# DeltaNet scan: the inverse built in 32x32 blocks, block transposes on VectorE, block substitution for the last join

## The chip, the cores and the metric

The kernel runs on one NeuronCore of a Trainium2 chip. The metric is device time in microseconds (us) of one execution. The engines are named as in the profile: PE (TensorE matmul), PEld (TensorE's weight loads, which overlap PE), DVE (VectorE), ACT (ScalarE), POOL (GpSimd), SP (SyncE, which here issues DMAs).

## What is computed

Two layers of a hybrid block act on 1024 latent and 256 context tokens of width 1024. Each has four groups of heads side by side (windowed attention, DeltaNet, retention, latent attention), an output projection and an MLP. Only the DeltaNet group is touched. The reference computes it per head and per direction in chunks:

```python
def _delta_update(s, w_i, u_i, kt_i, gl_i):
    v_new = u_i - jnp.einsum('bhcd,bhde->bhce', w_i, s)
    s_new = s * jnp.exp(gl_i)[..., None, None] + jnp.einsum('bhcd,bhce->bhde', kt_i, v_new)
    return s_new, v_new

# gated_delta_chunked, per chunk:
decay = jnp.exp(jnp.where(incl, g_cum[..., :, None] - g_cum[..., None, :], -jnp.inf))
a_mat = jnp.where(strict, jnp.einsum('bhncd,bhnsd->bhncs', kb, k) * decay, 0.0)
lhs = a_mat + jnp.eye(c_, dtype=a_mat.dtype)
rhs = jnp.concatenate([kb * jnp.exp(g_cum)[..., None], v * beta], axis=-1)
wu = lax.linalg.triangular_solve(lhs, rhs, left_side=True, lower=True)
# scan over chunks:
s_new, v_new = _delta_update(s, w_i, u_i, kt_i, gl_i)
o_i = jnp.einsum('bhcd,bhde->bhce', qd_i, s) + jnp.einsum('bhcs,bhse->bhce', qk_i, v_new)
```

There are 4 heads of 64 channels and 2 directions. The kernel takes chunks of 128 tokens, so each layer has 10 chunks per direction (2 context, 8 latent).

## The kernel before

Each layer runs through phases separated by barriers of all engines; `dn_scan` is one of them. Every engine has its own `dn_scan`, and all of them walk one hand-written list, `scan_plan()` (line 590), of pieces (name, step `s_`, direction `q`, level `lv`). An engine issues its part of each piece in the order of that list and waits on semaphores (`u_...`) where it needs another engine's result. So the list is the order of the queue of every engine, and an instruction that waits holds all behind it on its engine.

A step handles one chunk for both directions and all four heads. For the two directions `q`:

- gsum (PE), arg (DVE, four `STT` at line 2439 with a mask), exp (ACT, line 1814): the decay matrix. gram (PE, line 1207): products k.k and q.k. at (DVE, lines 2448 and 2450): both times decay.
- first (POOL, lines 2852 and 2853), seed (PE): the start of the inverse of (I + A), held as two 64x64 diagonal blocks per head, as `lower` and as its transpose `upper`.
- five levels of y and u double the size of the solved blocks from 2 to 64. y (PE, line 1228; DVE masks the result at line 2453 into `step`) multiplies A with `lower`. u (PE) makes two products, line 1236 for `lower` and line 1239 for `upper`; ACT copies both back (lines 1819, 1821; at the last level line 1826 writes `inv`).
- x and z (PE, lines 1248 and 1259; ACT, lines 1832 and 1837) join the two 64x64 blocks into the full 128x128 inverse `inv`. The next step's y waits for it.
- keg (POOL), w (PE, line 1269; ACT, line 1841): the inverse times decayed keys. v (PE, lines 1275 to 1281): state times q, inverse times values, minus w times state. DVE scales both at lines 2456 and 2457.
- kept, kt (POOL), o (PE, lines 1288 and 1291), out (DVE, lines 2463 to 2465): state update and output, added into `d_o`.

The pieces w, v, o and out of step s run between the levels of step s+1, and gsum to first run a step ahead. All matmuls of the scan are f32; each leaves two records on PE and two on PEld. The blocks of the array that a matmul uses follow from its operands' partitions: y and u alternate between rows and columns 0 to 63 and 64 to 127.

Of the kernel before, what the change touches and what calls it, by code (L numbers as in the profile page):

```python
# [16 lines left out]
ALU = mybir.AluOpType  # L17
# [23 lines left out]
LEVELS = 7  # L41
SCAN_MASKS = 7
# [107 lines left out]
class Lane:  # L150
# [84 lines left out]
    "u_g", "u_arg", "u_dt", "u_gram", "u_first", "u_ymm", "u_ysb", "u_umm", "u_lower", "u_upper", "u_xmm", "u_xsb",  # L235
    "u_zmm", "u_full", "u_keg", "u_wmm", "u_wsb", "u_vmm", "u_vsb", "u_omm", "u_done", "u_at", "u_kt", "u_kept")]
# [5 lines left out]
def build(nc, d, book):  # L242

    with ExitStack() as ctx:
# [134 lines left out]
        levels, j1 = cut(Hn, j0, 2, SCAN_MASKS, 64)  # L379
# [20 lines left out]
        for q_ in range(2):  # L400
            b = {}
            for n_ in ("lower", "upper", "step", "first"):
                b[n_], r0_ = cut(ringf, r0_, H, 64)
            for n_ in ("at", "qkd", "inv"):
                b[n_] = []
                for _ in range(2):
                    half_, r0_ = cut(ringf, r0_, H, P)
                    b[n_].append(half_)
            for n_ in ("keg", "kt", "wt", "vn"):
# [180 lines left out]
        def scan_plan():  # L590
# [7 lines left out]

            both = lambda what, s_, lv=0: [(what, s_, 0, lv), (what, s_, 1, lv)]
            one = lambda what, s_, q: [(what, s_, q, 0)]  # L600
            plan = []
            for what in ("gsum", "arg", "exp", "gram", "at", "first"):
                plan += both(what, 0)
            plan += one("gsum", 1, 0) + both("seed", 0)
            for s_ in range(NT):
                late = lambda what, q: one(what, s_ - 1, q) if s_ else []
                soon = lambda what, q: one(what, s_ + 1, q) if s_ + 1 < NT else []
                then = lambda what, q: one(what, s_ + 2, q) if s_ + 2 < NT else []
                y, u = (lambda lv, w_=w_: both(w_, s_, lv) for w_ in "yu")
                plan += late("w", 0) + y(1) + late("w", 1) + late("kept", 0) + late("kept", 1) + soon("arg", 0)  # L610
                plan += late("v", 0) + soon("exp", 0) + u(1) + y(2) + late("o", 0) + both("keg", s_) + soon("gram", 0)
                plan += u(2) + late("out", 0) + soon("at", 0) + late("v", 1) + y(3) + soon("gsum", 1)
                plan += u(3) + soon("first", 0) + soon("arg", 1) + y(4) + soon("exp", 1) + late("o", 1) + soon("gram", 1)
                plan += u(4) + late("out", 1) + soon("at", 1) + y(5) + soon("first", 1) + u(5) + both("kt", s_)
                plan += then("gsum", 0) + soon("seed", 0) + [("x", s_, 0, 0)] + soon("seed", 1) + [("z", s_, 0, 0)]
            for what in ("w", "kept", "v", "o", "out"):
                plan += both(what, NT - 1)
            return plan

# [131 lines left out]
        def _(pe):  # L751
# [429 lines left out]
            def dn_scan():  # L1181
                blocks = [slice(0, 64), slice(64, P)]
                for what, s_, q, lv in scan_plan():
                    b, now, tile = sc[q], s_ % 2, scan_tiles[s_][q]
                    at_, inv, cols = b["at"][now], b["inv"][now], slice(tile * P, (tile + 1) * P)
                    pair, prod, tail = ps[:, q, :], ps[:, 2 + q, :], ps[:, 4 + q, :]
                    upper = b["first"] if lv == 1 else b["upper"]
                    of = lambda h: slice(h * 64, (h + 1) * 64)
                    if what == "gsum":

                        if s_:
                            pe.wait_ge(sems[f"u_at{1 - q}"], nth(f"u_at{1 - q}", s_ + q))
# [9 lines left out]
                    if what == "gram":  # L1202
                        pe.wait_ge(sems[f"u_arg{q}"], nth(f"u_arg{q}", s_ + 1))
# [4 lines left out]
                        m.then_inc(sems[f"u_gram{q}"], tally(f"u_gram{q}"))  # L1208
                    if what == "seed":
                        pe.wait_ge(sems[f"u_first{q}"], nth(f"u_first{q}", s_ + 1))  # L1210
                        if s_:
                            pe.wait_ge(sems[f"u_lower{q}"], nth(f"u_lower{q}", 6 * s_))
                            pe.wait_ge(sems[f"u_upper{q}"], nth(f"u_upper{q}", 5 * s_))
                        for h in range(H):
                            for r in blocks:
                                pe.matmul(pair[r, h * 64:(h + 1) * 64], b["first"][r, h, :], ident[r, r],
                                          start=(h == 0), stop=False, skip_group_check=True)
                        for r in blocks:
                            m = pe.matmul(pair[r, 256:512], ident[r, r], b["first"][r].rearrange("p h c -> p (h c)"),
                                          start=False, stop=False, skip_group_check=True)  # L1220
                        m.then_inc(sems[f"u_umm{q}"], tally(f"u_umm{q}"))
                    if what == "y":
                        if lv == 1 and s_:
                            pe.wait_ge(sems[f"u_full{q}"], nth(f"u_full{q}", s_))
                        pe.wait_ge(sems[f"u_lower{q}"], nth(f"u_lower{q}", 6 * s_ + lv))
                        for h in range(H):
                            for r in blocks:
                                m = pe.matmul(prod[r, of(h)], at_[r, h, r], b["lower"][r, h, :], start=True, stop=True, skip_group_check=True)  # L1228
                        m.then_inc(sems[f"u_ymm{q}"], tally(f"u_ymm{q}"))
                    if what == "u":  # L1230
                        pe.wait_ge(sems[f"u_ysb{q}"], nth(f"u_ysb{q}", 5 * s_ + lv))
                        if lv > 1:
                            pe.wait_ge(sems[f"u_upper{q}"], nth(f"u_upper{q}", 5 * s_ + lv - 1))
                        for h in range(H):
                            for r in blocks:
                                pe.matmul(pair[r, of(h)], upper[r, h, :], b["step"][r, h, :], start=False, stop=(lv == 5), skip_group_check=True)  # L1236
                        for h in range(H):
                            for r in blocks:
# [1788 lines left out]
```

## Time and profile before

| | us |
|---|---|
| median of 3 runs | 4048.92 (4048.8 to 4049.25) |
| the profiled execution | 4048.99 |
| its span | 4047.2 |
| scan of layer 0, from 766.1 to 1086.9 | 320.8 |
| scan of layer 1, from 2851.9 to 3172.3 | 320.4 |

The view by stretches gives the busy time of each engine in a stretch of time and, behind it, the number of instructions in the order PE, PEld, DVE, ACT, POOL (PE and PEld alone where it is asked for one line of matmuls), then the mean granted clock of TensorE (1.00 is full) and the DMA's share. The view in order of time merges instructions of one line that follow one another: start, length of the whole piece, engine, line, operation, count, and in brackets the idle time before it with what ended it. Since matmuls overlap, the time that a group takes from its queue is the distance from its start to the start of the next group.

### The profile page before, as it was taken

How to read it: one execution, taken by the hardware profiler on the slowest of the kernel's cores; microseconds unless marked ns; L12 is line 12 of the kernel's file. 1: busy time of each engine (PE TensorE's matmuls, PEld its weight loads, DVE VectorE, ACT ScalarE, POOL GpSimd, SP SyncE). 2: the span in 40 equal slices, each digit the busy share in tenths (PEclk: the TensorE clock that was granted, in tenths of full speed). 3: DMA queues.
4: the chain of work that ended last, by engine and by line, in shares of the span. 5: the costliest groups of instructions: out<-in, count | busy, mean ns of one | idle time of the engine just before them, and what ended most of it. 6: DMA issues, size and time to landing. Idle time of an engine off the chain costs nothing.

```text
span 4047.2 us, 75588 instructions
## 1 busy us (share of the span) xinstructions
PE 3825.9 (95%) x32478; PEld 3201.9 (79%) x32478; DVE 1951.6 (48%) x3457; ACT 1121.1 (28%) x2430; POOL 905.1 (22%) x659
## 2 busy tenths in 40 slices
PE   6999999899899999999998999999899899999997
PEld 5668888788787888888886668878788778888886
DVE  3455566444456333333357464565444564333446
ACT  3444242333413111111114452252333321000111
POOL 1000100122103333333322001100222034443442
PEclk8999999899899999999998999999999899999999
DMA  4230000100000101101111120001000101111111
GB/s 179 102 149 32 22 22 22 61 3 3 23 32 32 42 31 41 42 31 41 41 40 73 63 105 22 22 12 42 32 3 3 43 32 53 42 52 52 41 52 52
DMA packets 30518, 180.81 MB, mean 45 GB/s; under 512 B 2592, under 2 KB 7968, under 8 KB 15136
## 3 DMA queue, kind: packets, MB, share of 16 engines
q1 hardware_dynamic: 28944, 173.66, 11.7%
q8 instruction: 221, 3.62, 0.4%
q10 hardware_dynamic: 1296, 3.07, 0.2%
q14 instruction: 57, 0.47, 0.0%
HBM read 168.32 MB, written 8.39 MB: 44 GB/s over the span
## 4 chain that ended last, share of the span: by engine, by line
PE 85%; DVE 8%; ACT 4%; issue 2%; DMA 1%; POOL 1%; ACTq 0%; POOLq 0%; DVEq 0%; SPq 0%
PE ps L1364 37%; PE ps L768 9%; PE ps L778 8%; PE ps L803 4%; PE ps L901 3%; PE ps L1228 3%; PE ps L1236 2%; PE ps L1239 2%; PE ps L943 2%; PE ps L986 1%; PE ps L1317 1%; PE ps L1207 1%; PE ps L812 1%; PE ps L1291 1%; PE ps L1008 1%
## 5 line engine op out<-in xcount | busy, mean ns | idle before, releaser
L1364 PE MATMUL ps<-Yn_parts,ring_parts 128*128 128x512 f32 (+1 forms) x3888 | 798.9, 367 | 2.4 <-DVE Yn_parts L2610 2.1
L1364 PEld LDWEIGHTS ps<-Yn_parts,ring_parts 128*128 128x128 f32 x3888 | 671.2, 189 | 126.7 <-DVE Yn_parts L2610 5.4
L1364 PE MATMUL ps<-temp_parts,ring_parts 128*128 128x512 f32 (+1 forms) x2560 | 726.5, 369 | 5.0 <-DVE Hn_parts L2551 3.6
L2871 POOL TENSOR_TENSOR ring_parts<-ring,consts 128x2048 fp32r<-128x2048 f32 x62 | 286.5, 4621 | 1187.4 <-DMA ring<-in_ff 1187.4
L1364 PEld LDWEIGHTS ps<-temp_parts,ring_parts 128*128 128x128 f32 x2560 | 464.9, 189 | 88.0 <-DVE Hn_parts L2551 4.1
L768 PE MATMUL ps<-ring_parts,Xn_parts 128*128 128x256 f32 x2560 | 506.1, 293 | 24.1 <-DVE Hn_parts L2122 16.2
L2498 DVE SCALAR_TENSOR_TENSOR Xn<-ps,mods,Xn 128x256 f32<-128x256 f32 (+1 forms) x364 | 251.7, 692 | 574.2 <-PE ps L1364 504.3
L1364 PE MATMUL ps<-Hn_parts,ring_parts 128*128 128x512 f32 (+1 forms) x1280 | 471.4, 368 | 0.0
L768 PEld LDWEIGHTS ps<-ring_parts,Xn_parts 128*128 128x128 f32 x2560 | 418.4, 196 | 27.3 <-issue 22.6
L1926 ACT ACTIVATE Yn<-ps 128x256 f32<-128x256 f32 (+1 forms) x160 | 88.6, 554 | 1237.6 <-PE ps L1364 1237.6
L2609 DVE TENSOR_TENSOR Yn<-Yn 128x256 f32<-128x256 f32 (+1 forms) x160 | 191.3, 1196 | 402.7 <-ACT Yn_parts L1928 402.7
L768 PE MATMUL ps<-ring_parts,Hn_parts 128*128 128x256 f32 x1280 | 367.5, 287 | 0.0
L2872 POOL TENSOR_TENSOR ring_parts<-ring,ring_parts 128x2048 fp32r<-128x2048 f32 x62 | 291.7, 4704 | 4.9
L803 PE MATMUL ps<-consts,temp 128*128 128x128 f32 (+1 forms) x1416 | 231.1, 285 | 47.4 <-DVE temp L2151 15.7
L1364 PEld LDWEIGHTS ps<-Hn_parts,ring_parts 128*128 128x128 f32 x1280 | 241.6, 189 | 40.4
L803 PEld LDWEIGHTS ps<-consts,temp 128*128 128x128 f32 (+1 forms) x1416 | 162.9, 142 | 114.2 <-issue 54.7
L768 PEld LDWEIGHTS ps<-ring_parts,Hn_parts 128*128 128x128 f32 x1280 | 251.5, 197 | 0.8
L2453 DVE TENSOR_TENSOR ring<-ps,Hn 128x256 f32<-128x256 f32 x200 | 84.7, 423 | 228.3 <-PE ps L1228 226.6
L1819 ACT ACTIVATE ring<-ps 128x256 f32<-128x256 f32 x240 | 91.6, 382 | 331.6 <-PE ps L1239 302.2
L2610 DVE TENSOR_TENSOR Yn_parts<-Yn,Yn_parts 128x256 fp32r<-128x256 f32 (+1 forms) x160 | 179.5, 1122 | 5.5
L901 PE MATMUL ps<-Yn,temp 96*128 96x512 f32 (+1 forms) x400 | 153.7, 518 | 4.2 <-ACT temp L1640 2.7
L778 PE MATMUL ps<-Xn_parts,ring_parts 128*128 128x512 f32 (+1 forms) x576 | 153.6, 355 | 0.9 <-DVEq L211 0.9
(318 smaller groups left out, 5610.1 us busy)
## 6 DMA issues: line engine op xcount, KB each, us to landing
ring<-in_ff SPq DMA_DIRECT2D x64, 1024.0 KB, 4.7
ring<-in_ada SPq DMA_DIRECT2D x22, 2048.0 KB, 9.0
ring<-in_halves SPq DMA_DIRECT2D x28, 1024.0 KB, 4.8
Xn<-in_x SPq DMA_DIRECT2D x1, 5120.0 KB, 16.8
Hn<-in_ada SPq DMA_DIRECT2D x2, 2048.0 KB, 21.1
Xn<-in_x SPq DMA_DIRECT2D x2, 2048.0 KB, 18.5
kept_x<-Xn SPq DMA_DIRECT2D x4, 1024.0 KB, 4.5
Xn<-kept_x SPq DMA_DIRECT2D x1, 4096.0 KB, 15.5
```

The source lines that it names most:

```text
L768: m = pe.matmul(ps[:, bank, 0:256], (G_hi, H_lo)[a][:, k, t * P:(t + 1) * P], w[b][:, k, :], start=(k == 0 and part == 0), stop=(k == KT - ...
L778: m = pe.matmul(ps[:, bank, 0:hi - lo], w[a][:, k, j * P:(j + 1) * P], x[b][:, k, lo:hi], start=(k == 0 and part == 0), stop=(k == KT - 1 ...
L803: return pe.transpose(out, src, ident[0:rows, 0:rows])
L901: m = pe.matmul(m_flat[:, base + a:base + b], m_q[0:96, h, t * P:(t + 1) * P], m_k[0:96, h, a:b], start=True, stop=True, skip_group_check= ...
L1228: m = pe.matmul(prod[r, of(h)], at_[r, h, r], b["lower"][r, h, :], start=True, stop=True, skip_group_check=True)
L1364: m = pe.matmul(ps[:, bank, 0:hi - lo], w[a][:, k, j * P:(j + 1) * P], x[b][:, k, lo:hi], start=(k == 0 and part == 0), stop=(k == k_n - 1 ...
L1819: A(flat(b["lower"]), ps[:, q, 0:256], ACT.Copy).then_inc(sems[f"u_lower{q}"], tally(f"u_lower{q}"))
L2498: return STT(X[:, j, lo:hi], ps[:, bank, 0:hi - lo], mods[:, L, gate_ + j, which:which + 1], X[:, j, lo:hi], ALU.mult, ALU.add)
L2609: link(TT(u_, u_, u_, ALU.mult))
L2610: TT(U_lo[:, j, lo:hi], u_, U_hi[:, j, lo:hi].bitcast(F32), ALU.subtract).then_inc(sems["hidden"], tally("hidden"))
L2871: link(TT(by(half_hi[s]), by(half[s]), spread(ones, 1, HALF // P), ALU.mult))
L2872: TT(half_lo[s], half[s], half_hi[s].bitcast(F32), ALU.subtract).then_inc(sems["split"], tally("split"))
```

## The change

The 128x128 matrix of a chunk is now solved with 32x32 blocks. `level_masks` makes masks of 32 columns and five levels. Four levels of y and u remain, each with 16 matmuls of 32x32 per direction in place of 8 of 64x64. The four diagonal blocks of A are first packed by a new piece, pk (PE with ACT), and atm (POOL) multiplies them by the masks of all levels at once, so that y's result is only copied (ACT). u makes only `lower`; a VectorE transpose of 32x32 blocks makes `upper`. a and b (PE with ACT) join pairs of 32x32 blocks to 64x64; wide (DVE) writes the diagonal part. The second join to 128x128 is gone: reach takes state times k and state times q, the correction is subtracted from the values (DVE, then POOL), and x1, off, x2 do the substitution over the two 64x64 blocks directly on them. w, keg, and the inverse-times-value product are gone. arg moves from DVE to ACT (Relu with a bias and negative scale, then exp with scale -1); the triangle mask that it held is now applied by mask (POOL) to qkd. The accumulation into `d_o` moves from DVE to POOL (acc). `at` and `qkd` of direction 0 get a third buffer. The plan is written anew.

```diff
-LEVELS = 7
-SCAN_MASKS = 7
+LEVELS = 5
+SCAN_MASKS = LEVELS + 1
...
+    one = lambda what, s_, q, lv=0: [(what, s_, q, lv)] if 0 <= s_ < NT else []
+    part = lambda what, s_, q, heads=range(H): [i_ for h in heads for i_ in one(what, s_, q, h)]
     plan = []
+    for q in range(2):
+        plan += one("gsum", 0, q)
+    for q in range(2):
+        plan += part("arg", 0, q) + one("exp", 0, q) + one("gram", 0, q)
+    for q in range(2):
+        plan += part("at", 0, q) + one("qkd", 0, q) + one("mask", 0, q) + one("pk", 0, q) + one("atm", 0, q)
+    plan += one("gsum", 1, 0) + part("arg", 1, 0) + one("exp", 1, 0) + one("gram", 1, 0)
+    plan += both("start", 0) + both("seed", 0) + both("kept", 0) + both("kt", 0)
     for s_ in range(NT):
+        late = lambda what, q, s_=s_: one(what, s_ - 1, q)
+        soon = lambda what, q, s_=s_: one(what, s_ + 1, q)
+        then = lambda what, q, s_=s_: one(what, s_ + 2, q)
+        plan += y(1) + late("x1", 0) + late("x1", 1) + part("at", s_ + 1, 0)
+        plan += u(1) + late("off", 0) + late("off", 1) + soon("qkd", 0) + soon("mask", 0)
+        plan += y(2) + soon("pk", 0) + late("x2", 0) + late("x2", 1) + soon("gsum", 1)
+        plan += u(2) + part("arg", s_ + 1, 1, (0, 1)) + late("tail", 0) + soon("atm", 0)
+        plan += y(3) + part("arg", s_ + 1, 1, (2, 3)) + late("tail", 1)
+        plan += u(3) + soon("exp", 1) + soon("gram", 1)
+        if s_:
+            plan += both("kept", s_)
+        plan += y(4) + late("acc", 0) + late("acc", 1) + part("at", s_ + 1, 1, (0, 1)) + one("reach", s_, 0)
+        plan += u(4) + part("at", s_ + 1, 1, (2, 3)) + one("reach", s_, 1)
+        plan += [("a", s_, 0, 0)] + both("wide", s_) + soon("start", 0) + soon("qkd", 1) + soon("mask", 1) + soon("pk", 1) + soon("atm", 1) + then("gsum", 0)
+        plan += [("b", s_, 0, 0)] + soon("seed", 0) + part("arg", s_ + 2, 0) + soon("start", 1)
+        plan += soon("seed", 1) + then("exp", 0) + then("gram", 0)
+        if s_:
+            plan += both("kt", s_)
+    for what in ("x1", "off", "x2", "tail", "acc"):
     return plan
+blocks32 = [slice(32 * n_, 32 * n_ + 32) for n_ in range(4)]
+blocks64 = [slice(0, 64), slice(64, P)]
+def pair_of(q, c):
+    return (2 * c, 2 * c + 1) if q == 0 else (2 * c + 1, 2 * c)
+def kept_back(q):
+    return 3 - q
...
+            if what == "pk":
+                pe.wait_ge(sems[f"u_kq{q}"], nth(f"u_kq{q}", 2 * s_ + 2))
+                for r in blocks32:
+                    m = pe.matmul(ps[r, scan_banks(s_, q)[0], 0:P], ident[r, r], at_[r, :, r], start=True, stop=True, skip_group_check=True)
+                m.then_inc(sems[f"u_pk{q}"], tally(f"u_pk{q}"))
...
             if what == "y":
+                if lv == 1:
+                    pe.wait_ge(sems[f"u_staged{q}"], nth(f"u_staged{q}", 2 * s_ + 2))
+                    if s_:
+                        pe.wait_ge(sems[f"u_inv{q}"], nth(f"u_inv{q}", 2 * s_))
+                else:
+                    pe.wait_ge(sems[f"u_lower{q}"], nth(f"u_lower{q}", 4 * s_ + lv - 1))
                 for h in range(H):
+                    for r in blocks32:
+                        m = pe.matmul(prod[r, of32(h)], atm[r, lv, of32(h)], b["lower"][r, h, :], start=True, stop=True, skip_group_check=True)
                 m.then_inc(sems[f"u_ymm{q}"], tally(f"u_ymm{q}"))
             if what == "u":
+                pe.wait_ge(sems[f"u_ysb{q}"], nth(f"u_ysb{q}", 4 * s_ + lv))
                 if lv > 1:
+                    pe.wait_ge(sems[f"u_upper{q}"], nth(f"u_upper{q}", 4 * s_ + lv - 1))
                 for h in range(H):
+                    for r in blocks32:
+                        upper = atm[r, 0, of32(h)] if lv == 1 else b["upper"][r, h, :]
+                        m = pe.matmul(pair[r, of32(h)], upper, b["step"][r, h, :], start=False, stop=(lv == 4), skip_group_check=True)
+                m.then_inc(sems[f"u_umm{q}"], tally(f"u_umm{q}"))
+            if what == "a":
+                for q_ in range(2):
+                    pe.wait_ge(sems[f"u_lower{q_}"], nth(f"u_lower{q_}", 4 * s_ + 4))
+                    for h in range(H):
+                        for c in range(2):
+                            near, far = (blocks32[n_] for n_ in pair_of(q_, c))
+                            m = pe.matmul(ps[far, 2 + q_, of32(h, P)], sc[q_]["at"][s_ % kept_back(q_)][near, h, far],
+                                          sc[q_]["lower"][near, h, :], start=True, stop=True, skip_group_check=True)
+                    m.then_inc(sems[f"u_lmm{q_}"], tally(f"u_lmm{q_}"))
...
+            if what == "reach":
+                if s_:
+                    pe.wait_ge(sems[f"u_tv{q}"], nth(f"u_tv{q}", 4 * s_))
+                else:
+                    pe.wait_ge(sems["u_packed1"], nth("u_packed1", 1))
+                for a_ in (1, 0):
+                    for j in range(2):
+                        m = pe.matmul(tail[:, 256 * a_ + j * P:256 * a_ + (j + 1) * P], raw[:, 2 * a_ + j, cols], b["S"][:, j, :],
+                                      start=True, stop=True, skip_group_check=True)
+                m.then_inc(sems[f"u_tmm{q}"], tally(f"u_tmm{q}"))
+            if what == "x1":
+                pe.wait_ge(sems[f"u_r{q}"], nth(f"u_r{q}", s_ + 1))
+                pe.wait_ge(sems[f"u_inv{q}"], nth(f"u_inv{q}", 2 * s_ + 2))
                 for h in range(H):
+                    m = pe.matmul(tail[have, of(h)], inv[have, h, :], b["r"][have, of(h)], start=True, stop=True, skip_group_check=True)
+                m.then_inc(sems[f"u_tmm{q}"], tally(f"u_tmm{q}"))
...
+            if what == "arg":
+                if lv == 0:
+                    act.wait_ge(sems[f"u_g{q}"], nth(f"u_g{q}", s_ + 1))
+                    if s_:
+                        act.wait_ge(sems[f"u_kq{q}"], nth(f"u_kq{q}", 2 * s_))
+                at_col = gate_col(q, tile)
+                m = A(b["ex"][:, lv, :], ps[:, scan_banks(s_, q)[lv // 2], (lv % 2) * P:(lv % 2 + 1) * P], ACT.Relu,
+                      bias=g_tok[:, lv, at_col:at_col + 1], scale=-1.0)
+                if lv == H - 1:
+                    m.then_inc(sems[f"u_decay{q}"], tally(f"u_decay{q}"))
...
+            if what == "y":
+                act.wait_ge(sems[f"u_ymm{q}"], nth(f"u_ymm{q}", 4 * s_ + lv))
+                A(flat(b["step"]), ps[:, 2 + q, 0:P], ACT.Copy).then_inc(sems[f"u_ysb{q}"], tally(f"u_ysb{q}"))
...
+            if what == "x1":
+                act.wait_ge(sems[f"u_tmm{q}"], nth(f"u_tmm{q}", 5 * s_ + 2))
+                A(b["vn"][have], ps[have, 4 + q, 0:256], ACT.Copy, scale=-1.0).then_inc(sems[f"u_x1{q}"], tally(f"u_x1{q}"))
 ...
+            if what == "u":
+                dve.wait_ge(sems[f"u_lower{q}"], nth(f"u_lower{q}", 4 * s_ + lv))
+                dve.transpose(flat(b["upper"]), flat(b["lower"])).then_inc(sems[f"u_upper{q}"], tally(f"u_upper{q}"))
+            if what == "wide":
+                dve.wait_ge(sems[f"u_upper{q}"], nth(f"u_upper{q}", 4 * s_ + 4))
+                if s_:
+                    dve.wait_ge(sems[f"u_tmm{q}"], nth(f"u_tmm{q}", 5 * s_ - 1))
+                TT(b["inv"].rearrange("p h (n c) -> p h n c", n=2), spread(b["upper"], 2, 2), spread(in_pair, 1, H), ALU.mult)\
+                    .then_inc(sems[f"u_wide{q}"], tally(f"u_wide{q}"))
...
+            if what == "off":
+                dve.wait_ge(sems[f"u_tmm{q}"], nth(f"u_tmm{q}", 5 * s_ + 3))
+                TT(b["r"][off], tail[off, 256:512], b["r"][off], ALU.add).then_inc(sems[f"u_tv{q}"], tally(f"u_tv{q}"))
...
+            if what == "mask":
+                pool.wait_ge(sems[f"u_kq{q}"], nth(f"u_kq{q}", 2 * s_ + 2))
+                TT(qkd, qkd, spread(tri[:, q, :], 1, H), ALU.mult).then_inc(sems[f"u_mask{q}"], tally(f"u_mask{q}"))
+            if what == "atm":
+                pool.wait_ge(sems[f"u_packed{q}"], nth(f"u_packed{q}", s_ + 1))
+                if s_ >= 2:
+                    pool.wait_ge(sems[f"u_ymm{q}"], nth(f"u_ymm{q}", 4 * s_ - 4))
+                link(TT(hd(atm[:, 0, :]), b["pk"], spread(levels[:, q, 0, :], 1, H), ALU.mult))
+                TT(hd(atm[:, 0, :]), hd(atm[:, 0, :]), spread(levels[:, q, LEVELS, :], 1, H), ALU.add).then_inc(sems[f"u_staged{q}"], tally(f"u_staged{q}"))
+                TT(atm[:, 1:LEVELS, :].rearrange("p l (h c) -> p l h c", h=H), spread(b["pk"], 1, LEVELS - 1), spread(levels[:, q, 1:LEVELS, :], 2, H), ALU.mult)\
+                    .then_inc(sems[f"u_staged{q}"], tally(f"u_staged{q}"))
+            if what == "reach":
+                pool.wait_ge(sems[f"u_tv{q}"], nth(f"u_tv{q}", 4 * s_ + 1))
+                TT(b["r"], kv_tok[:, tile, 256:512], b["r"], ALU.subtract).then_inc(sems[f"u_r{q}"], tally(f"u_r{q}"))
...
```

The scan plan of the kernel before is line 599 to 618; `late`, `soon` and `then` mean that a piece belongs to the step before, the next and the one after.

## Rows read from the trace of the kernel before

**Rows 1.** The page's first part: busy us (share of the span) xinstructions of each engine.

```profile
PE 3825.9 (95%) x32478; PEld 3201.9 (79%) x32478; DVE 1951.6 (48%) x3457; ACT 1121.1 (28%) x2430; POOL 905.1 (22%) x659
```

**Rows 2.** Busy time by stretch: length, then us and instructions of each engine, clock, DMA.

```profile
766.10:1086.90 320.80, 301.01 (x6640) 267.55 (x6640) 141.04 (x400) 113.89 (x320) 79.53 (x122) 0.98 0.01 3
...
832.50:863.70 31.20, 29.81 (x664) 26.48 (x664) 14.01 (x40) 11.40 (x33) 7.89 (x12) 1.00 0.01 3
...
767.50:777.70 10.20, 7.73 (x61) 5.54 (x62) 5.05 (x17) 1.64 (x3) 5.25 (x8) 0.50 0.00 1
...
2851.90:3172.30 320.40, 300.64 (x6640) 267.39 (x6640) 141.21 (x400) 113.87 (x320) 79.48 (x122) 0.98 0.01 3
```

**Rows 3.** In order of time, one steady step of layer 0: start, us, engine, line, operation.

```profile
832.50 0.78 ACT L1837 ACTIVATE ring<-ps 64x256 f32<-64x256 f32 x2 [0.67 <-PE ps L1259]
...
838.60 0.55 PEld L1239 LDWEIGHTS ps<-ring 64*64 64x64 f32 x16
...
839.07 0.55 PEld L1228 LDWEIGHTS ps<-ring 64*64 64x64 f32 x16
...
839.77 0.54 PEld L1228 LDWEIGHTS ps<-ring 64*64 64x64 f32 x16 [0.15 <-ACT ring L1819]
...
840.38 0.31 PEld L1288 LDWEIGHTS ps<-Yn 128*64 128x64 f32 x8
...
840.77 0.97 PEld L1291 LDWEIGHTS ps<-Yn,ring 128*128 128x128 f32 x8
...
841.80 0.73 PEld L1207 LDWEIGHTS ps<-temp 64*128 64x128 f32 x8
...
842.87 0.54 PEld L1236 LDWEIGHTS ps<-ring 64*64 64x64 f32 x16 [0.33 <-issue]
...
863.68 0.38 ACT L1837 ACTIVATE ring<-ps 64x256 f32<-64x256 f32 x1 [0.67 <-PE ps L1259]
```

**Rows 4.** Stretches of 25 ns at L1073 and L1160 alone, and of 0.48 us at seed.

```profile
420.32:420.35 0.03, 0.02 (x4) 0.02 (x4) 1.00 0.00 0
...
743.53:743.55 0.03, 0.02 (x4) 0.03 (x4) 1.00 3.83 1638
...
860.59:861.07 0.48, 0.48 (x30) 0.48 (x28) 0.00 (x0) 0.24 (x1) 0.48 (x2) 1.00 0.00 0
```

**Rows 5.** Groups by line and shape: count | busy us, mean ns of one | idle before.

```profile
L1228 PE MATMUL ps<-ring 64*64 64x64 f32 x3200 | 125.3, 221 | 2.2 <-ACT ring L1819 1.2
...
L1684 ACT ACTIVATE temp<-ps 128x128 f32<-128x128 f32 x20 | 5.5, 277 | 47.2 <-PE ps L803 47.2
...
L1589 ACT ACTIVATE temp<-ps,params 128x128 f32<-128x128 f32 x60 | 19.6, 362 | 11.5 <-PE ps L803 11.5
...
L2165 DVE TENSOR_SCALAR temp<-temp 128x128 f32<-128x128 f32 x20 | 4.2, 218 | 2.9 <-PE ps L803 2.9
...
L2448 DVE SCALAR_TENSOR_TENSOR ring<-ps,Hn 128x128 f32<-128x128 f32 x160 | 45.0, 343 | 15.2 <-DVE temp L2465 10.3 <-PE ps L1207 4.9
...
L2450 DVE TENSOR_TENSOR ring<-ps,Hn 128x512 f32<-128x512 f32 x40 | 27.1, 679 | 0.0
...
L2456 DVE TENSOR_TENSOR Yn<-ps,Hn 128x256 f32<-128x256 f32 x40 | 17.0, 424 | 70.1 <-PE ps L1281 70.1
...
L2853 POOL TENSOR_TENSOR ring<-ring,Hn 128x256 f32<-128x256 f32 x40 | 29.0, 725 | 3.1
```

**Rows 6.** In order of time, the first step of layer 0: weight loads of a seed.

```profile
774.91 0.93 PEld L1216 LDWEIGHTS ps<-consts,ring 64*64 64x64 f32 x16 [0.22 <-issue]
```

**Rows 7.** In order of time, layer 0: the first y, the last z and the end.

```profile
777.93 0.70 PEld L1228 LDWEIGHTS ps<-ring 64*64 64x64 f32 x16
...
1076.72 0.78 ACT L1837 ACTIVATE ring<-ps 64x256 f32<-64x256 f32 x2 [0.94 <-PE ps L1259]
...
1086.37 0.42 DVE L2465 TENSOR_TENSOR temp<-temp,Yn 128x256 f32<-128x256 f32 x1
```

More of the change, by code:

```diff
@@ L401, in build @@
             b = {}
-            for n_ in ("lower", "upper", "step", "first"):
-                b[n_], r0_ = cut(ringf, r0_, H, 64)
-            for n_ in ("at", "qkd", "inv"):
+            for n_ in ("lower", "upper", "step", "pk"):
+                b[n_], r0_ = cut(ringf, r0_, H, 32)
+            b["inv"], r0_ = cut(ringf, r0_, H, 64)
+            b["atm"] = []
+            for _ in range(2):
+                half_, r0_ = cut(ringf, r0_, LEVELS, P)
+                b["atm"].append(half_)
+            for n_ in ("at", "qkd"):
                 b[n_] = []
@@ L613, in scan_plan @@
[L613 to L616, printed above, removed]
+                late = lambda what, q, s_=s_: one(what, s_ - 1, q)
+                soon = lambda what, q, s_=s_: one(what, s_ + 1, q)
@@ L1211, in dn_scan @@
                         if s_:
[L1212 to L1217, printed above, removed]
@@ L1252, in dn_scan @@
-                    if what == "z":
-                        for q_ in range(2):
-                            pe.wait_ge(sems[f"u_xsb{q_}"], nth(f"u_xsb{q_}", s_ + 1))
-                            pe.wait_ge(sems[f"u_upper{q_}"], nth(f"u_upper{q_}", 5 * s_ + 5))
-                        for h in range(H):
-                            for q_ in range(2):
-                                have, off = blocks[q_], blocks[1 - q_]
-                                m = pe.matmul(ps[have, 2 + q_, of(h)], sc[q_]["step"][off, h, :], sc[q_]["inv"][now][off, h, off],
-                                              start=True, stop=True, skip_group_check=True)
-                                if h == H - 1:
-                                    m.then_inc(sems[f"u_zmm{q_}"], tally(f"u_zmm{q_}"))
@@ new lines, in dn_scan @@
+                    if what == "x2":
+                        pe.wait_ge(sems[f"u_tv{q}"], nth(f"u_tv{q}", 4 * s_ + 2))
+                        for h in range(H):
+                            m = pe.matmul(tail[off, of(h)], inv[off, h, :], b["r"][off, of(h)], start=True, stop=True, skip_group_check=True)
+                        m.then_inc(sems[f"u_tmm{q}"], tally(f"u_tmm{q}"))
+                    if what == "tail":
+                        pe.wait_ge(sems[f"u_tv{q}"], nth(f"u_tv{q}", 4 * s_ + 3))
@@ new lines, in dn_scan @@
+                    if what == "qkd":
+                        if s_ >= back:
+                            dve.wait_ge(sems[f"u_tmm{q}"], nth(f"u_tmm{q}", 5 * (s_ - back) + 5))
+                        TT(by_half(qkd), gram[:, :, 0, :, :], by_half(b["ex"]), ALU.mult).then_inc(sems[f"u_kq{q}"], tally(f"u_kq{q}"))
+                    if what == "start":
+                        dve.wait_ge(sems[f"u_staged{q}"], nth(f"u_staged{q}", 2 * s_ + 1))
+                        if s_:
+                            dve.wait_ge(sems[f"u_lmm{q}"], nth(f"u_lmm{q}", 2 * s_ - 1))
+                        dve.transpose(flat(b["lower"]), b["atm"][s_ % 2][:, 0, :]).then_inc(sems[f"u_start{q}"], tally(f"u_start{q}"))
```

285 lines of the change are left out of this document (113 added, 172 removed).

## The prediction

> **What bounds the kernel now.** I read the page first: PE is busy for 95% of the span [rows 1]. That share is over all stages, so I went to the stretches next. The change touches only the two DeltaNet scans. They fill 320.8 us (layer 0) and 320.4 us (layer 1), 641 of 4047 us, and in both PE is busy for 94% at a granted clock of 0.98 [rows 2]. In a steady stretch from one evacuation of z (ACT L1837) to the next, 832.50 to 863.68, a step takes 31.2 us, of which PE is busy for 29.8, DVE for 14.0, ACT for 11.4 and POOL for 7.9 [rows 2, 3]. So inside the scan the end is set by PE's own queue, and the other three have more than half of the step free. What I need from the trace is therefore how long PE takes for each kind of group, start to start, because a matmul's own duration overlaps the next one's.
>
> **PE's prices, from starts in one step [rows 3].** Each matmul of f32 data leaves two records. Sixteen 64x64 records, which alternate between two diagonal blocks of the array, take 839.07-838.60 = 0.47 us: 29 ns a record, 58 ns a record on one block. The o part of one direction (L1288, L1291) takes 841.80-840.38 = 1.42; its eight 128x128 records take 841.80-840.77 = 1.03, with the change of shape behind them. A gram (L1207) takes 842.87-841.80 = 1.07, with the change of shape behind it. A y group that is followed by another shape takes 840.38-839.77 = 0.61 in place of 0.47, so a change of shape costs about 0.15. A gsum has half of a gram's columns: (1.07-0.15)/2+0.15 = 0.6. At these prices a step before has ten y 4.7, ten u (two products each) 9.3, o 2.8, gram 2.1 and gsum 1.2, 20.1 of the 29.8 us; seeds, x, z, w and v are the rest.
>
> **The unknown price: 32x32 matmuls.** Nothing in the scan before is 32x32. Three rows bound it [rows 4]. L1073 uses four blocks of 32 rows: four matmuls start within 25 ns. L1160 uses four blocks of 32 columns: again four within 25 ns. And where seed and x overlap on all four 64x64 blocks, 28 weight loads fall into 0.48 us, 17 ns a record. So different blocks of the array run side by side, in rows and in columns, and a start itself costs about 6 ns (25/4). A 32-column record on one block should take half of the 58 ns, and four blocks at once give 7 to 8 ns a record. Low end 0.22 us for a y or u group of 32 records, high end 0.93 (the 29 ns of the 64x64 pairs), with 17 ns (0.54) between them. I take 0.26, nearest to L1073, which has the same four row blocks. Pk and seed (8 records of 128 columns) I take at 0.3.
>
> **PE's list after the change, one step, both directions.** Removed: a fifth level of y and u, the second product of every u (the transpose that DVE now makes), x and z as 64x64, w, and the inverse-times-value part of v. Added: y and u as 32x32, 16 x 0.26 = 4.2 (before 14.0). a and b, 4 x 0.26 = 1.0. pk and seed, 4 x 0.3 = 1.2. x1, off and x2, six groups of eight 64x64 records on one block each, 6 x 0.47 = 2.8. reach, 2 x 1.03 = 2.1. tail as o before, 2.8. gsum 1.2, gram 2.1. Twelve further changes of shape, 12 x 0.15 = 1.8. Sum 19.2 us against 29.8. PE no longer fills the step, so what matters next is where its queue, which is strictly in the order of the plan, stops for others.
>
> **The new waits.** I walked the order of the plan with durations of ACT 0.28 (128x128 copy, L1684), 0.36 (with a bias operand, L1589), DVE 0.34 (L2448), 0.68 (L2450), 0.42 (L2456), POOL 0.73 per 256 elements (L2853) and 0.2 us from the last start of a PE group to its reader (one 64x64 record lasts 0.22, L1228) [rows 5]. Four places wait:
> The gram two steps ahead, directly behind b and the seeds, needs the four arg activations, which now are ACT's and stand behind b's four evacuations: 0.43+0.04+4x0.28+4x0.36 = 3.0 us after b begins, while PE has about 1.0 of b and seeds: 2.1 (y of the next step and everything else queue behind it).
> pk of direction 0 stands ahead of x2 and needs qkd, behind both off additions on DVE: 0.42+0.42+0.68 against PE's off and y groups: 0.6.
> pk of direction 1 stands ahead of b and needs qkd of direction 1, behind DVE's reach (2x0.42), wide (2x0.42), start (0.3) and qkd (0.68): 2.7 plus drain 0.2 and leftovers of two transposes, less PE's a group: 2.5. This holds b, thus the inverse, thus the next step.
> gsum behind it needs pk's evacuation by ACT: 0.6.
> Sum 5.8, so 25.0 at full clock. The 32x32 transposes by VectorE aren't in the trace; their nearest rows are 0.22 (L2165) and 0.34 (L2448), and I take 0.29. The eight of the levels come 2 to 4 us before they are needed; three lie on the third wait, so the ends move the step by -0.2 to +0.2. ACT's 38 and DVE's 36 instructions of a step, at 0.28 to 0.68 us each, come to about 13 and 12 us; POOL's, by elements, to about 13 (mask 2x1.3, atm 2x2.2, eight others at 0.7). All stay below 25: none becomes the bound, and what POOL newly does (mask, atm, reach's subtraction, acc) is covered by PE's middle levels as long as a step is longer than that. The change of ring buffers moves no DMA.
>
> **The clock.** The granted clock was 0.50 from 767.5 to 777.7, where PE was busy for 7.7 of 10.2 us with pauses for the others before and inside, and the sixteen 64x64 weight loads of a seed took 0.93 us there, against 0.55 for sixteen of y at full clock [rows 2, 3, 6]. The steps after that, with PE busy without a break, ran at 1.00. The new step has a stretch of some 5 us around b with little on PE in every step, so I expect the clock to fall to the 1.2 GHz level there and to come back during the first levels. The price runs from 0 to 3 us a step (the 3 us of gram, y, x1 and u after the pause taking twice as long); I take half: 1.5. Step: 26.5 us.
>
> **The sum.** Per layer: start to first y 12.7 (before, 766.1 to 777.9: 11.8; plus mask and atm on POOL); first step without late parts 26.5-6 = 20.5; seven at 26.5 = 185.5; the ninth without gsum, arg and gram ahead 23.0; the last without any look-ahead 17.5; the last tail 8.5 (before, 1076.7 to 1086.8: 10.1) [rows 2, 7]. Together 267.7 against 320.7, -53.0 a layer, -106 in all. The profiled execution took 4048.99 us for a span of 4047.2, the median of the runs is 4048.92, so the sum needs no shift: 4049-106 = 3943 us. Each us of the step is 20 us.
>
> **Rivals.**
> *Fewer waits (faster).* ACT's and DVE's short instructions overlap their predecessor, so the first and third wait shrink by about 3 us in all, and the clock stays at 1.00: step 22, 3853 us. For: the rows give how long one such instruction lasts, not how closely independent ones follow. Against: what PE waits for is the end of the last one.
> *Clock low for half of PE's work.* 19.2/2 = 9.6 us more, of which the 5.8 of waits hide somewhat over half: step 30, 4013 us.
> *PE takes 32x32 records no faster than 64x64 pairs (slower than before).* At 29 ns a record, y, u, a and b cost 11.7 more: step 36.7, with the clock kept up by a busy PE, 4147 us. It decides from a step of 31.8, that is 6.8 us over 25.0, or 12 ns more for each of the 576 records: about 20 ns a record. For: no row shows a longer run than 17 ns a record. Against: [rows 4].
> The Trainium skill has a rule that speaks for this rival: "TensorE: Matmul & The Clock Gate", Part 1, says that the starts of matmuls don't come closer than about 25 ns however small they are. By that figure a group of 32 would be 0.8 us, the step about 34 and the time, as an estimate, about 4100. The traces disagree with it where blocks differ: four starts in 25 ns [rows 4].
> *No change.* It needs a step of 31.4 to 32.2 by chance of the above.
>
> **Chances.** Forecast (step 24 to 29) 62%, fewer waits 15%, low clock 11%, slow 32x32 9%, no change 3%. A measurement of this kernel can tell about 0.2% (8 us) from no change. From the same cases: faster 87%, same 3%, slower 10%. The range reaches from the fewer-waits case to past the low-clock case, 3855 to 4030, and leaves out the slow 32x32 case and the best end.
>
> **What would show it.** Right: in a steady step, y and u groups start 0.2 to 0.3 us apart; PE's idle time is released by ACT (arg before gram, pk before gsum) and by DVE (qkd before pk), most of it around b; PE busy falls to about three quarters; the clock row of the scan falls below 0.98. Wrong: a y group of 0.5 us or more; idle PE in front of u or y in the middle levels (then the copies or transposes are the chain); POOL as releaser of start, y or x1.

## The result, and the profile after

The changed kernel takes 4020.18 us (median of 5 runs, 4013.82 to 4027.17), the one before 4049.25 (4048.8 to 4050.17) beside it: a ratio of 0.9929, 95% interval 0.9914 to 0.9943. So it is faster by 0.7%, which is clear of the noise, and inside the range, but by 29 us in place of 106. The profiled execution took 4017.37 us for a span of 4015.6.

The busy times of the page (of all stages), beside [rows 1]:

```profile
PE 3729.1 (93%) x33918; PEld 3083.6 (77%) x33918; DVE 1924.5 (48%) x3377; ACT 1116.2 (28%) x2550; POOL 986.6 (25%) x731
```

By stretch, as in [rows 2]: the scan of layer 0 (first gsum to last instruction), a long and a short step of it (from one first y to the next), the scan of layer 1:

```profile
768.90:1078.30 309.40, 256.07 (x7360) 210.09 (x7358) 125.13 (x360) 111.58 (x380) 120.83 (x160) 0.72 0.01 3
835.29:868.50 33.21, 28.95 (x739) 24.02 (x737) 12.62 (x36) 11.20 (x38) 12.07 (x16) 0.60 0.02 3
901.64:928.10 26.46, 21.69 (x739) 17.38 (x737) 12.43 (x36) 11.12 (x38) 12.07 (x16) 0.89 0.02 4
2837.20:3140.90 303.70, 251.40 (x7360) 206.83 (x7358) 125.04 (x360) 111.30 (x380) 120.81 (x160) 0.73 0.01 3
```

The two scans take 309.4 and 303.7 us, before 320.8 and 320.4. The granted clock of the scan, 0.98 before, is 0.72. The same step, with the same instructions, takes 26.5 us at a clock of 0.89 and 33.2 at 0.60. From one first y to the next, the second to eighth step of layer 0 take 26.6, 33.2, 33.2, 26.5, 28.9, 33.2 and 28.0 us: mean 29.9 (layer 1: 26.2 to 33.2, mean 29.7).

PE in order of time in the ninth step, which has no gsum and gram two steps ahead, from the end of the levels to the next first y (L1242 gram, L1265 y, L1302 reach, L1274 u, L1282 a, L1247 pk, L1292 b, L1254 seed), as in [rows 3] but for the matmuls:

```profile
1030.38 0.75 PE L1274 MATMUL ps<-ring 32*32 32x32 f32 x64
1031.06 1.14 PE L1242 MATMUL ps<-temp 64*128 64x256 f32 x8
1032.13 0.75 PE L1265 MATMUL ps<-ring 32*32 32x32 f32 x64
1032.81 1.16 PE L1302 MATMUL ps<-Hn,temp 128*128 128x128 f32 x8
...
1038.58 0.31 PE L1247 MATMUL ps<-ring,consts 32*32 32x128 f32 x4 [2.31 <-DVE ring L2498]
...
1041.21 0.65 PE L1254 MATMUL ps<-ring,consts 32*32 32x128 f32 x8 [1.65 <-DVE ring L2503]
```

Both directions of a y or u, 64 records, take 0.68 us to the next group (1031.06-1030.38, 1032.81-1032.13). Less 0.15 for the change of shape that is 0.27 a group, forecast 0.26. Around b PE is idle for 2.31 us, then for 1.65.

What PE waited for in layer 0, from 780 to 1080 us (us in total, times, longest):

```profile
PE ps L1247 <- DVE ring L2498: 20.9, 10, 2.3
PE ps L1242 <- ACT Hn L1857: 11.1, 9, 1.4
PE ps L1265 <- issue: 4.6, 7, 1.3
PE ps L1234 <- ACT ring L1868: 3.5, 9, 0.4
PE ps L1274 <- issue: 2.9, 4, 1.3
PE ps L1254 <- DVE ring L2503: 2.5, 4, 1.6
```

The places are those forecast: pk behind qkd, gram behind arg, gsum behind pk's evacuation. Seed behind start, and pauses that nothing in the profile explains ("issue") inside y and u groups, are new. Groups of layer 0 that the prediction had priced from [rows 5] (us, mean ns of one):

```profile
L2506 DVE STREAM_TRANSPOSE ring<-ring 128x128 f32<-128x128 f32 x80 | 23.8, 306 | 44.1 <-ACT ring L1874 42.2
...
L2511 DVE TENSOR_TENSOR ring<-ring,Hn 128x256 f32<-128x256 f32 x20 | 12.8, 682 | 0.0
```

The transposes take 0.306 us (forecast 0.29). Wide takes 12.8/20 = 0.64 (forecast 0.42).

### The profile page after: what moved, and what is told of

Same layout as the page of the kernel before. It is cut to its first block, busy times and chain, and to the rows that moved or that the text cites. A ratio compares the mean times of both kernels' runs of the same rounds, so it can differ in the third digit from the quotient of the medians.

```text
span 4015.6 us, 78630 instructions
## 1 busy us (share of the span) xinstructions
PE 3729.1 (93%) x33918; PEld 3083.6 (77%) x33918; DVE 1924.5 (48%) x3377; ACT 1116.2 (28%) x2550; POOL 986.6 (25%) x731
## 4 chain that ended last, share of the span: by engine, by line
PE 83%; DVE 9%; ACT 5%; issue 2%; DMA 1%; POOL 1%; ACTq 0%; DVEq 0%; POOLq 0%; SPq 0%
PE ps L1402 38%; PE ps L803 9%; PE ps L813 8%; PE ps L838 4%; PE ps L936 3%; PE ps L978 2%; PE ps L1242 2%; PE ps L1274 2%; PE ps L1265 1%; PE ps L1329 1%; PE ps L1302 1%; PE ps L1355 1%; PE ps L1021 1%; PE ps L1043 1%; PE ps L847 1%
## 5 line engine op out<-in xcount | busy, mean ns | idle before, releaser
L1402 PE MATMUL ps<-temp_parts,ring_parts 128*128 128x512 f32 (+1 forms) x2560 | 727.1, 370 | 5.0 <-DVE Hn_parts L2616 3.6
L2563 DVE SCALAR_TENSOR_TENSOR Xn<-ps,mods,Xn 128x256 f32<-128x256 f32 (+1 forms) x364 | 251.8, 692 | 572.7 <-PE ps L1402 501.7
L2271 DVE TENSOR_REDUCE small<-ps 128x1 f32<-128x1280 f32 x72 | 98.8, 1373 | 79.2 <-PE ps L936 78.9
L813 PE MATMUL ps<-temp_parts,ring_parts 128*128 128x512 f32 (+1 forms) x448 | 129.5, 374 | 0.0
## 6 DMA issues: line engine op xcount, KB each, us to landing
Hn<-in_ada SPq DMA_DIRECT2D x2, 2048.0 KB, 20.7
```

The costliest lines, as they stand in the source:

```text
L813: m = pe.matmul(ps[:, bank, 0:hi - lo], w[a][:, k, j * P:(j + 1) * P], x[b][:, k, lo:hi], start=(k == 0 and part == 0), stop=(k == KT - 1 ...
L1402: m = pe.matmul(ps[:, bank, 0:hi - lo], w[a][:, k, j * P:(j + 1) * P], x[b][:, k, lo:hi], start=(k == 0 and part == 0), stop=(k == k_n - 1 ...
L2271: dve.tensor_reduce(rowneg[:, at_], m_flat[:, base:base + latent_keys(t) * P], AX.X, ALU.min).then_inc(sems["rowmax"], tally("rowmax"))
L2563: return STT(X[:, j, lo:hi], ps[:, bank, 0:hi - lo], mods[:, L, gate_ + j, which:which + 1], X[:, j, lo:hi], ALU.mult, ALU.add)
```

## The experiments

The first theory was that PE's idle time around b lets the clock fall, and that the clock is the whole loss. Its rivals: the 32x32 work itself keeps the clock low ("small blocks", later "narrow"), or the waits themselves are the loss. A filler is matmuls of constants into PSUM columns that nobody reads; "wide" work is matmuls over more of the array than 32x32 blocks (the DVE piece wide is something else). Each kernel was timed against the one before, which took 4049 to 4051 us each time; the clock and the length are those of layer 0's scan in the profiled execution.

| | us | ratio, 95% interval | scan, us | clock |
|---|---|---|---|---|
| the change | 4020.2 | 0.9914 to 0.9943 | 309.4 | 0.72 |
| e1_fill_gaps | 3962.0 | 0.9764 to 0.9797 | 283.0 | 0.89 |
| e4_fill_elsewhere | 4081.8 | 1.0065 to 1.0098 | 337.8 | 0.71 |
| e2_qkd_early | 4031.3 | 0.9933 to 0.9966 | 316.3 | 0.62 |
| e3_qkd_early_gram_late | 3953.3 | 0.9735 to 0.9784 | 268.3 | 0.82 |
| e7_gram_late | 4017.4 | 0.9893 to 0.9926 | 308.7 | 0.68 |
| e8_qkd_fill_y1 | 3974.8 | 0.9797 to 0.9829 | 284.7 | 0.81 |
| e5_fill_narrow | 4123.8 | 1.0158 to 1.0219 | 354.9 | 0.74 |
| e9_fill_blocks | 3985.7 | 0.9821 to 0.9857 | 296.2 | 0.82 |
| e6_qkd_gram_fill | 3917.6 | 0.9657 to 0.9689 | 251.8 | 0.93 |
| e10_fill_gsum_only | 3933.5 | 0.9677 to 0.9723 | 261.6 | 0.87 |

**Filler in the idle stretches, and the same filler elsewhere.**

```diff
+if what == "fill":
+    for n_ in range(lv):
+        pe.matmul(ps[:, q, 384:512], ident, ident, start=True, stop=True, skip_group_check=True)
 # e1, in the plan
-... + soon("pk", 1) + ...
+... + soon("fill", 0, 8) + soon("pk", 1) + ...
-... + then("gram", 0)
+... + then("fill", 0, 5) + then("gram", 0)
 # e4 instead (into bank 2)
-u(3) + ...
+u(3) + soon("fill", 1, 13) + ...
```

> Thirteen f32 matmuls of 128x128 into unused PSUM columns are put into the two longest idle stretches of PE in a steady step: eight ahead of pk of direction 1, five ahead of gram two steps ahead (0.26 us each at full clock; they end later than the idle times of 2.3 and 1.4 us by little). Theory 'idle PE around b lets the clock fall': the scan stretch goes from a granted clock of 0.71 to 0.95 or more, the mean step from 29.2 to about 26.4 us, the time to about 3970 us, although PE has more to do. Rival 'small blocks': the 32x32 work itself lets the clock fall, so the clock stays below 0.8 and the time is 4020 to 4050 us. Rival 'waits': the loss is in the length of the waits, and the time stays at 4020 us or more whatever the clock does.

> The same thirteen matmuls as in the one that fills the two idle stretches, but all behind u of level 3, where PE does not wait. Theory 'idle PE around b lets the clock fall': the idle stretches stay, the clock still falls in each step (0.65 to 0.8), and the time grows by the filler, 18 x 3.4 to 5 us: 4080 to 4110 us. Rival 'small blocks': what matters is how much wide work PE has in a step, wherever it is; the clock rises as much as in the other kernel with filler.

In e1 the second filler opens an accumulation in a bank where a seed is open, which changes the inverse; PE's instructions are otherwise those of the change. A step of e1 (busy time by stretch):

```profile
935.00:960.30 25.30, 22.65 (x780) 19.18 (x776) 12.31 (x36) 11.13 (x38) 12.08 (x17) 1.00 0.01 4
```

With 3.3 us more of work the step takes 25.3 us, less than any of the change's seven middle steps in either layer (26.2 and more), at a clock of 1.00; the time falls by 58 us against the change. The clock of the whole scan, 0.89, is less than the 0.95 expected. Behind u of level 3 the same work costs 62 us. So the loss hangs on the clock, and on what PE does around b. "Waits" as the whole of the loss falls, and so does "small blocks" in the form that the amount of wide work decides.

**The waits taken away by order alone.**

```diff
 # e2
-u(4) + part("at", s_ + 1, 1, (2, 3)) + one("reach", s_, 1)
-[("a", ...)] + both("wide", s_) + soon("start", 0) + soon("qkd", 1) + soon("mask", 1) + soon("pk", 1) + ...
+u(4) + part("at", s_ + 1, 1, (2, 3)) + soon("qkd", 1) + soon("mask", 1) + one("reach", s_, 1)
+[("a", ...)] + both("wide", s_) + soon("start", 0) + soon("pk", 1) + ...
 # e7 (e3 is both)
-soon("seed", 1) + then("exp", 0) + then("gram", 0)
+soon("seed", 1)
-y(1) + late("x1", 0) + ...
+y(1) + (soon("exp", 0) + soon("gram", 0) if s_ else []) + late("x1", 0) + ...
```

> The product qkd of direction 1 (and its mask) goes ahead of DVE's reach, wide and start pieces, so that pk of direction 1 no longer waits for it; no work is added or left out. Theory 'idle PE around b lets the clock fall': the 2.1 us wait at pk goes, 18 steps x 2.1 = 38 us, and the clock rises with it; 3920 to 3980 us, scan clock 0.8 or more. Rival 'waits': only the wait goes, 3982 us, clock as it was (0.71). Rival 'next in line': the wait moves to seed, which waits for start on DVE; over 4000 us.

> As the one with qkd early, and exp and gram of direction 0 two steps ahead move behind the y of the next step's first level, so that this y is not queued behind ACT's arg. Theory 'idle PE around b lets the clock fall': both waits go (2.1 + 1.2 us a step) and the clock is 0.9 or more; step 23 to 25 us, 3870 to 3940 us. Rival 'waits': 18 x 3.3 = 59 us less, 3960 us, clock about 0.71. Rival 'next in line': DVE gets at of direction 0 later, its transposes for u queue behind it, and y of the middle levels waits; 3980 us or more.

> Exp and gram of direction 0 two steps ahead move behind the y of the next step's first level, qkd stays where it is: the half of the two moves that the earlier kernel with both left untold. Theory 'idle': the 2.3 us wait at pk stays, so the clock falls in each step as in the changed kernel; 18 steps x 1.2 us of the arg wait are gained, about 4000 us. Theory 'narrow': what matters is that wide work (gram, x1) follows soon after b; the clock comes back within a few us in each step, 0.9 in the scan, 3960 to 3985 us.

E2 comes out at 4031. That is what "next in line" has (over 4000), and the wait at seed does grow, from 2.5 to 8.4 us, but the time isn't lost there: the wait at pk went as meant, and the waits are shorter in all. PE's waits in e2, layer 0:

```profile
PE ps L1254 <- DVE ring L2503: 8.4, 18, 1.4
PE ps L1234 <- ACT ring L1868: 6.2, 9, 0.7
PE ps L1242 <- ACT Hn L1857: 2.5, 8, 0.5
PE ps L1247 <- DVE ring L2498: 2.0, 9, 0.2
```

19.1 us together, in place of the change's 38.0 in the same four (20.9+11.1+3.5+2.5), and still it is slower than the change by some 11 us, because the clock now falls at b in every step and stays there (three stretches in a row of e2, from the seeds behind b to y of the fourth level, then to the next seeds, then again):

```profile
892.60:916.50 23.90, 22.96 (x560) 18.79 (x556) 8.00 (x24) 8.13 (x27) 8.71 (x12) 0.50 0.01 3
916.50:923.40 6.90, 5.63 (x203) 4.63 (x192) 5.24 (x13) 3.08 (x12) 3.56 (x5) 0.99 0.01 2
923.40:947.20 23.80, 22.89 (x551) 18.67 (x546) 7.89 (x24) 8.15 (x27) 8.73 (x12) 0.50 0.01 3
```

PE is busy for 22.96 of 23.90 us, 96%, and the clock stays at 1.2 GHz; it returns behind the two tails and gram and is lost again at the next b. The middle steps take 30.8 to 31.3 us. So idle time doesn't explain why the clock stays low. The Trainium skill, "TensorE: Matmul & The Clock Gate", Part 1, says that "the default state is throttled, and activity releases the throttle"; in this stretch 23 us of matmuls did not.

The change itself shows both returns. Of its sixteen falls at b ahead of the second to ninth steps (both layers), the clock was back after 6.8 us in eight, after 10.2 in two, and after 23.9 to 30.7 in six. Two of them, with the same groups of work behind b:

```profile
831.45:855.35 23.90, 22.62 (x540) 18.64 (x544) 7.66 (x24) 8.25 (x28) 8.15 (x11) 0.50 0.01 3
896.30:903.13 6.83, 5.51 (x131) 3.65 (x127) 1.44 (x5) 3.40 (x11) 3.26 (x6) 0.50 0.01 2
```

They differ in where among these groups the clock fell. In the eight short ones the gram that follows b began 2.5 to 3.8 us after the fall, in the six long ones 1.8, 2.2, 3.9, 4.3, 4.5 and 7.5 us after it. In e2, with less waiting ahead of that gram, it began 0.5 to 1.8 us after each of the sixteen falls, and all sixteen took 23.9 us. This is read from the traces afterwards; no run shifted the fall alone, so it isn't shown to be the cause.

E7 shortens the arg wait but leaves the other: 4017, no gain, clock 0.68. Its "narrow" expectation missed, and "idle" was too hopeful by 17 us. Of the runs that only move work, e3 with both moves alone brings the clock up, to 0.82, and is 67 us faster. E3's 3953 us misses "idle" (at most 3940, clock 0.9) and lies 7 us from "waits" (3960), though not at the clock of 0.71 that this had: what the order alone gained and what the clock gave back aren't separated in e3.

**Wide work where PE doesn't wait, and narrow work where it does.**

```diff
 # e8: e2, and (into bank 0, start=False)
-y(1) + late("x1", 0) + ...
+y(1) + soon("fill", 0, 4) + late("x1", 0) + ...
 # e5: as e1 with 118 and 73 of
+r = blocks32[n_ % 4]
+pe.matmul(ps[r, 0, 384:416], ident[r, r], ident[r, r], start=False, stop=False, ...)
 # e9: as e1, each of 8 and 5 being
+for r in blocks32:
+    pe.matmul(ps[r, 0, 384:512], ident[r, r], ident[r, :], start=False, stop=False, ...)
```

> Qkd early alone (which ran at a clock of 0.61 with little idle time of PE), and four 128x128 matmuls into unused PSUM columns behind the y of level 1, where PE does not wait (1.0 us at full clock). Theory 'narrow': the clock, which there stays at 1.2 GHz for 24 us of narrow work in each step, is back soon after b; step 24.5 to 26 us, 3940 to 3970 us, although PE has 1 us more to do. Theory 'idle': no idle time is filled, so the clock stays at 0.61 and the time is 18 x 2 us longer, about 4070 us.

> The two idle stretches of PE (ahead of pk of direction 1 and of gram two steps ahead) are filled as long as in the kernel with thirteen wide matmuls, but with 32x32 ones on four blocks of the array: 118 and 73 of them, about 2.1 and 1.3 us at 8.8 ns a record. Theory 'idle': with PE as busy as there, the clock is as high (0.95 or more in the scan) and the time about 3960 us. Theory 'narrow': what counts is not only that PE is busy but with how wide work; the clock stays below 0.85 and the time is 4000 us or more.

> The two idle stretches of PE are filled once more, eight and five times, each time with four matmuls of 128 columns on the four diagonal 32x32 blocks of the array in place of one of 128x128. They run side by side, so a set should last about as long as one wide matmul (0.26 to 0.35 us), and 52 more matmuls a step don't strain PE's supply of instructions as the 191 small ones did. Theory 'idle': PE is as busy as with the wide filler, so the clock is 0.95 or more in the scan and the time 3960 to 3980 us. Theory 'narrow': a quarter of the rows and columns in use doesn't do; clock below 0.85, 4010 us or more.

E8 adds 1 us of work a step to e2, fills no wait, and is 57 us faster. A step of e8:

```profile
860.50:885.60 25.10, 21.04 (x744) 17.35 (x744) 12.91 (x37) 11.15 (x39) 12.31 (x17) 1.00 0.01 4
```

It is 5 us above "narrow" and 95 below "idle". Fourteen of its fifteen falls at b ahead of the second to ninth steps ended after 3.4 to 10.2 us, one after 23.9. In ten of them gram began 0.1 to 1.8 us after the fall, as in e2, and nine of these ten were over after 3.4 or 6.8 us: so here it is the added work behind b that brought the clock back soon. That it has to be wide isn't shown, since no run put as much narrow work in this place. E5 fits the ranges of "narrow", but doesn't decide as it was meant to: with 191 more small matmuls a step PE paused in the filler itself, with nothing in the profile to wait for (layer 0, first line of its waits), so the stretches were not filled:

```profile
PE ps L1228 <- issue: 31.2, 20, 2.5
```

E9 is the cleaner form. Its time lies between the two expectations, its clock, 0.82, under the 0.85 of "narrow". Around a, fill, pk, gsum and seed it holds the clock; then, in six of the sixteen steps, it is lost later, in pk or x2 behind y of level 2 (e9, a stretch of each):

```profile
873.50:881.80 8.30, 7.06 (x209) 5.36 (x209) 3.20 (x8) 4.20 (x14) 5.34 (x7) 1.00 0.02 4
...
887.20:900.80 13.60, 13.60 (x323) 11.68 (x320) 4.61 (x14) 3.66 (x14) 5.25 (x8) 0.51 0.02 4
```

So for the fall at b, idle time was enough of a cause: filled even with 32x32 blocks, the clock held there at fifteen of the sixteen b ahead of the ninth step's. What lets it fall in e9's second level (PE had pauses of 0.7 to 1.2 us there) stays open.

**Both together.**

```diff
 # e6: e3, and (bank 1, start=False); e10 has the middle one alone
+soon("fill", 0, 2) + soon("pk", 1) + ... + then("fill", 0, 3) + then("gsum", 0)
+soon("fill", 0, 2) + soon("seed", 1)
```

> Qkd early and gram late, and seven 128x128 matmuls into unused PSUM columns in the short waits that are left around b: two ahead of pk of direction 1, three ahead of gsum two steps ahead, two ahead of seed of direction 1 (1.8 us a step at full clock; the waits there are 0.3 to 0.7, 0.7 and 0.3 to 0.6 us). Theories 'idle' and 'narrow' agree: the clock no longer falls around b (0.98 or more in the scan), the step is 23 us and the time 3910 to 3925 us. Rival 'cost': the filler lengthens the step by as much as the clock gives back; 3950 us or more.

> Qkd early and gram late, with only the three 128x128 matmuls ahead of gsum (0.8 us a step, where PE waits 0.7 us for ACT), without those ahead of pk and seed. If three wide matmuls around b are enough for the clock, it is 0.98 or more in the scan and the step 0.3 to 0.5 us shorter than with seven: 3908 to 3915 us. If the amount counts, the clock falls in some of the steps: 0.93 to 0.97, 3920 to 3945 us.

A steady step of e6, and its way through b (L1227 is the filler):

```profile
873.40:896.60 23.20, 21.68 (x758) 18.14 (x750) 12.90 (x36) 10.90 (x40) 12.23 (x17) 1.00 0.02 5
```

```profile
891.86 0.60 PE L1285 MATMUL ps<-ring 32*32 32x32 f32 x32
892.39 0.71 PE L1227 MATMUL ps<-consts 128*128 128x128 f32 x4
893.03 0.42 PE L1250 MATMUL ps<-ring,consts 32*32 32x128 f32 x8
893.38 0.94 PE L1227 MATMUL ps<-consts 128*128 128x128 f32 x6
894.25 0.71 PE L1237 MATMUL ps<-Hn,consts 64*128 64x128 f32 x8
```

The step is 23.2 us with the filler in it, the clock 1.00 in both layers from the second step to the eighth (0.74 and 0.73 in the first), the time 3917.6: 103 us below the change, 134 below the kernel before. E10, with the three ahead of gsum alone, loses the clock in three of the sixteen steps from the second to the ninth and is 16 us slower. The intervals overlap a little, and one of its four runs, at 3919.2, is as fast as e6: that the other four matmuls are worth something is likely, and whether by their number or by their places isn't separated.

## Why the prediction was right or wrong

**Right: what bounds it and PE's list.** Forecast 19.2 us of PE a step; in e6, at full clock, PE is busy for 21.7 with about 2 of filler. The price of 32x32 records was 0.26 a group and measured 0.27. The rival that they are no faster than 64x64 pairs is out: 0.68/64 is 10.6 ns a record with the change of shape (21 ns a matmul of two records), where it needed about 20 a record. The figure of 25 ns of the Trainium skill ("TensorE: Matmul & The Clock Gate", Part 1), cited there, does not hold for different 32x32 blocks here. One reading was off without touching the sum: of the 28 weight loads in 0.48 us [rows 4] four had begun before that stretch, so it is 20 ns a record in place of 17.

**Right in the main: the waits.** Forecast 2.5 at pk of direction 1, 2.1 at gram, 0.6 at gsum; measured 2.3, 11.1/9 = 1.2, and 0.4. The 0.6 at pk of direction 0 hardly shows. In their place came (2.5+4.6+2.9)/9 = 1.1 a step of seed and "issue" pauses. Together 5.0, forecast 5.8; that the sums are so close is in part luck, since 1.1 of the 5.0 lies where none was forecast. ACT, DVE and POOL were busy for 11.2, 12.6 and 12.1 us of the long step, forecast 13, 12 and 13. At full clock the step of 25.0 stands: in e1, whose filler takes the place of the two long waits, the second to eighth steps of layer 1 take 176.5/7 = 25.2 at a clock of 1.00:

```profile
2848.30:3024.76 176.46, 161.03 (x5337) 135.46 (x5335) 86.57 (x252) 77.79 (x266) 84.60 (x112) 1.00 0.02 4
```

**Wrong: the size of the clock's term.** The prediction saw the mechanism (little on PE around b, the clock falls there) and priced it at 0 to 3 us a step by letting the clock come back "during the first levels"; it took 1.5. Measured: the mean step was 29.9 and 29.7, so the term was 4.8 over 25.0. The failing step of the reasoning is the return. It was taken from [rows 2, 6], where the clock rose at 777.7 and then stayed up under 64x64 and 128x128 work; nothing in the trace before showed 32-wide work at the low clock. In the change the clock falls at every b from the first step's on. Where it came back in the first level, the step takes 26.2 to 28.9 us (forecast 26.5); but in three of the seven middle steps of each layer it stays at 1.2 GHz through most of the step, which then takes 33.1 to 33.2. So what failed is that the clock would be back in the first levels every time; what decides between the two is not shown (see e2).

Where the miss lies, for layer 0 and 1: start to first y 14.0 and 13.8 (forecast 12.7); first step 25.9 and 24.3 (20.5; the clock was 0.70 and 0.78 there, but e6, with the gram moved out of this step, has 21.3 and 20.7 at 0.74 and 0.73, so the share of the clock is not separated); seven steps 209.5 and 207.8 (185.5); the ninth 23.5 and 24.4 (23.0); the last with its tail 36.5 and 33.5, at a clock of 0.55 and 0.60 (26.0). Together 309.4 and 303.7 against 267.7: 78 us for both layers, of which the fourteen middle steps have 46, and 3943+78 = 4021.

**Rivals.** What came was "clock low for half of PE's work", step 30 and 4013 us, which had 11%; the time lies inside the stated range only because the range reached past this rival. "Fewer waits" needed a step of 22 and 3853 us; the nearest run is e6, with the waits moved or filled and the clock held, at 23.2 and 3918.

## What to carry to other kernels

Splitting matmuls into small blocks can buy PE time and lose it to the clock: price the new work at both clock levels, and read from a trace behind what work, and how reliably, the clock came back before assuming that it does. When a wait is removed and the time doesn't follow, look at the granted clock by stretch before looking for a new wait. A few wide dummy matmuls in waits on PE that are there anyway cost little, and here, with a better order, they brought the gain from 29 to 134 us.

## What the runs showed of the hardware

- PE busy for 96% of 23.9 us with f32 matmuls, most of them 32x32 and 64x64, stayed at a granted clock of 0.50 (e2).
- In the change the clock came back 6.8 or 10.2 us after ten of sixteen falls and 23.9 to 30.7 us after six, with the same groups of work behind them; in e2 23.9 us after all sixteen.
- Four 128x128 matmuls a step (1.0 us) behind the first y took the scan's clock from 0.62 to 0.81 (e2 to e8); 3.3 us of it behind u of level 3 left it at 0.71, in the change 0.72 (e4).
- PE paused in the middle of groups of small matmuls with nothing to wait for: 7.5 us a layer in the change (up to 1.3 us each), 31.2 us at one line with 10652 in place of 7360 records in the scan (e5, up to 2.5 us).
- A VectorE transpose of 32x32 blocks over 128x128 f32 took 0.306 us.
